# Second block's output product, residual, last norm, transposes and router: from one pass over both tiles to one pass per tile

## The chip, the cores and the metric

The kernel runs on one core of one Trainium2 chip. The metric is the device time of one execution in microseconds (us); a run counts with its median over several executions. TensorE (PE), VectorE (DVE), ScalarE (ACT), GpSimd (POOL) and SyncE (SP) each work through an instruction list of their own in order and meet through semaphores. Most of the work hands tiles between them.

## The reference, cut to what matters

Two model blocks follow one another on 512 tokens of width 1024. The second block, from its merged mixer output on, is what the change touches:

```
# second_block, one layer; x is [1, 512, 1024] float32
merged = sigmoid(gate_conv) * conv_o + sigmoid(gate_attn) * attn_o
h = h + merged @ w_out                        # output product and residual
xt = rms_norm_2(h, g_ffn)                     # the last norm ahead of the experts
g_logits = xt @ w_group + b_group             # router: 4 group columns
e_logits = xt @ w_expert + b_expert           # and 32 expert columns
...                                           # top 2 of 32 experts, each 1024 -> 512 -> 1024
```

`w_out` is [1024, 1024]; the router has 36 columns in all.

## The kernel before, in words

**Tiles and halves.** The 512 tokens are four tiles of 128. Two tiles make a half (`hf` 0 and 1), and every stage of the blocks is run by half. `H(t)` is the residual of tile `t` (128 tokens by 1024), `GC(k)` holds the merged mixer output transposed (128 channels by the 256 tokens of a half, k = 0..7), `r0` holds normed rows, and `GA(k)` the transposed normed rows that the router reads. `bank(b)` is one of eight PSUM banks of 512 columns.

**Interleaving.** `second_pe`, `second_act` and `second_dve` are generators, one for each engine. Half 0 of the second block runs beside the last pair of tiles of the first block's expert layer: `rows_pe` and its fellows walk through 64 steps, and `segs_at` says at which step each generator moves on to its next `yield`. On PE each of these steps (in the part at issue) is a sum of gathered rows (`sum_pe`, line 562, 16 or so matmuls), and POOL gathers 128 rows of `peer_v` by an indirect DMA for each (line 457), four to a step, into a ring of slots that the sums free. Half 1 of the second block runs alone after it (`for _ in second_pe(pe, 1): pass`), and after that come the routing (from line 2217) and the experts (from line 2335), which run in phases: no engine enters a phase before all have left the last.

**Order by name.** Each engine's steps have names in hand-written lists: `C_PE`, `C_ACT` and `C_DVE`. A step's place in its list is the value that its engine's semaphore has when it is done; `on_pe("o3")` waits for that value.

**The part at issue**, before: PE makes four output products `o0`..`o3` of 128x512 (8 matmuls each) in the order (columns 0 to 511, tile 0), (the same columns, tile 1), (columns 512 to 1023, tile 0), (these, tile 1). DVE adds each to `H` (line 1983). When a tile's second product is added (`h0`, `h1`), ACT squares and sums the row and takes the root (`rms`, lines 1777 and 1779); DVE takes the reciprocal (line 1884) and writes the normed row to `r0` (line 1991, `xn0`, `xn1`). PE waits for `xn1` and transposes both tiles together: 16 transposes of 128x128 into four banks (`turned_both`, line 1627). ACT copies them out in eight copies of 256 columns (line 1872, `x7_0`..`x7_7`). PE waits for the last copy and makes both tiles' router products (`lg0`, `lg1`), and DVE adds the bias (line 1996).

**Weights.** Weights are streamed by SP in the order of the list `stream`, 2 MB pieces for the most part, alternately into the two slots `w0` and `w1` (`wslot(i)`). SP issues piece i when piece i-2 has been used for the last time: `C_LAST_USE` names the PE step for each piece of a half. `w_out` is two pieces, columns 0 to 511 (called A below) and 512 to 1023 (B). A is issued when the last product of `w_attn_out` is done (`ma3`), B when the last one of `w_conv_out` is (`mc3`). The next half's first two pieces (of `w_in`) follow A and B. In half 1 one expert's down weights are put ahead of B in the same queue (`EXPERT_AT`, `expert_weights_sp`), and more expert weights stand behind it:

```
EXPERT_AT = {marks["attn_out1"]: 0, marks["out21"]: 1, marks["out21"] + 1: 2}
...
                if i in EXPERT_AT:
                    expert_weights_sp(sp, [EXPERT_AT[i]])
...
                sp.dma_start(dst, src).then_inc(sem(f"w_ready{i % 2}"), 16)
```

Matrix products go through the helper `matmuls`, whose line 196 is what the profile shows for them. One float32 matmul of the kernel gives two records there, one transpose gives one.

Of the kernel before, what the change touches and what calls it, by code (L numbers as in the profile page):

```python
# [7 lines left out]
ALU = mybir.AluOpType  # L8
ACT = mybir.ActivationFunctionType
AXIS_X = mybir.AxisListType.X  # L10

P = 128
D = 1024
# [15 lines left out]
def build_program(nc, A, out):  # L29
    ctx = ExitStack()  # L30
    with ctx:
# [49 lines left out]
        def wslot(i):  # L81
            return W[i % 2]
# [1497 lines left out]
        def by_head2(order):  # L1580
# [10 lines left out]
        C_PE = [(four("turn") + ["g0", "g1", "a0", "a1", "q0", "q1", "kk", "vv"] + heads  # L1591
                 + four("ma") + ["ln1", "ln2"] + four("mc") + four("o") + four("turn7_") + ["lg0", "lg1"])
                for heads in (apart(PE_HEADS), beside(PE_HEADS, 1))]
        C_ACT = [(["sq5_0", "rms5_0", "sq5_1", "rms5_1", "sq6_0", "rms6_0", "sq6_1", "rms6_1"] + [f"x6_{k}" for k in range(KD)]
                  + ["g0", "g1", "q0", "q1", "kk", "vv"] + heads + four("ysq") + ["lnrms", "silu"]
                  + ["sq7_0", "rms7_0", "sq7_1", "rms7_1"] + [f"x7_{k}" for k in range(KD)])
                 for heads in (apart(ACT_HEADS), [n for n in beside(ACT_HEADS, 3) if n[:2] != "ga"]
                               + four("ga") + four("sc"))]
        C_DVE = (["h5_0", "h5_1", "raw0", "raw1", "cv0", "cv1"]
                 + by_head2(((1, "sec"), (0, "fs"), (0, "fm"))) + four("ma") + ["cen", "nrm"] + four("mc")  # L1600
                 + ["h0", "h1", "xn0", "xn1", "lg0", "lg1"])
        c_pe, c_act, c_dve = by_half(C_PE), by_half(C_ACT), numbered(C_DVE)
        C_LAST_USE = ["g1", "a1", "q1", "vv", "gc1", "gc3", "ga1", "ga3", "ma3", "mc3", "o1", "o3"]

# [13 lines left out]
        def second_pe(pe, hf):  # L1618
# [135 lines left out]
            for g in range(4):  # L1754
                i = first + 10 + g // 2
                if g % 2 == 0:
                    w_arrived(pe, i)
                did(matmuls(pe, bank(g), lambda k: GC(k, (g % 2) * P, P), lambda k: wslot(i)[:, k, :], KD))
                yield
            yield  # L1760
            on_dve("xn1")
            turned_both(lambda t, k: mem("r0", t * D + k * P, P))
            yield
            on_act("x7_7")
            for i in range(2):
                did(matmuls(pe, bank(i, 0, NL), lambda k: GA(k, i * P, P), ROUTER, KD))
            yield

        def second_act(act, hf):
# [95 lines left out]
            for i in range(2):  # L1865
                on_dve(f"h{i}")
                rms(i, "7_", "r0")
            yield
            for k in range(KD):
                if k % 2 == 0:  # L1870
                    on_pe(f"turn7_{k // 2}")
                did(act.activation(GA(k), bank(k // 2, (k % 2) * 256, 256), ACT.Copy))
            yield
            yield
# [4 lines left out]
        def second_dve(dve, hf, link):  # L1879
# [93 lines left out]
            for b in range(4):  # L1973
# [5 lines left out]
                yield  # L1979
            for g in range(4):  # L1980
                t = 2 * hf + g % 2
                on_pe(f"o{g}")
                add = dve.tensor_tensor(H(t, 512 * (g // 2), 512), H(t, 512 * (g // 2), 512), bank(g), ALU.add)
                if g >= 2:
                    did(add)
                yield
            for i in range(2):
                t = 2 * hf + i
                on_act(f"rms7_{i}")
                rstd(t)  # L1990
                did(dve.scalar_tensor_tensor(mem("r0", t * D, D), H(t), mem("cols", COL_RSTD + t, 1), FFN_ROW, ALU.mult, ALU.mult))
            yield
            yield
            for i in range(2):
                on_pe(f"lg{i}")
                did(dve.tensor_tensor(LOGITS(2 * hf + i), bank(i, 0, NL), RB, ALU.add))
            yield
# [321 lines left out]
        def expert_weights_sp(sp, qs):  # L2319
            for q in qs:  # L2320
# [7 lines left out]
                if q == 5:  # L2328
                    sp.wait_ge(sem("c_dve"), c_dve(1, "lg1"))
                    sp.wait_ge(sem("c_act"), c_act(1, "x7_7"))  # L2330
                if q >= len(EREGS):
# [228 lines left out]
```

## Time and profile before

| what | value |
|---|---|
| median of 3 runs | 3019.09 us (3007.09 to 3020.22) |
| profiled execution, its own time | 3044.59 us |
| its span | 3042.9 us |
| PE busy in the span | 2276.7 us (75%) |
| DVE, ACT, POOL busy | 1551.5, 473.8, 1098.1 us |
| mean granted TensorE clock | 0.848 of full speed |

The profile is one execution under the hardware profiler, whose span runs from the first to the last record. Times in the rows count from the span's start. A number in square brackets behind a timeline row is how long the engine sat idle before it, and what ended that.

### The profile page before, as it was taken

What the parts mean: (1) busy time and instruction counts of PE and PEld (TensorE: products, weight loads), DVE (VectorE), ACT (ScalarE), POOL (GpSimd) and SP (SyncE); (2) the same over time, 40 slices, a digit from 0 to 9 for tenths busy, and PEclk for the clock granted to TensorE, in tenths of its full rate; (3) what the DMA queues carried; (4) which work ended last, traced back from release to release, by engine and by line L of the source; (5) the groups of instructions that cost most, each with busy time, mean ns of one, the idle gap of its engine ahead of it and who ended that gap; (6) DMA issues with size and microseconds to landing.
All of it is one profiled execution on the core that took longest, in us unless ns stands there. A gap on an engine that the chain in (4) does not pass through costs nothing.

```text
span 3042.9 us, 29697 instructions
## 1 busy us (share of the span) xinstructions
PE 2276.7 (75%) x11113; PEld 1284.6 (42%) x11113; DVE 1551.5 (51%) x3350; ACT 473.8 (16%) x786; POOL 1098.1 (36%) x1229
## 2 busy tenths in 40 slices
PE   6999485595557596457887267667798789999995
PEld 4676354342325342325643145333376533333331
DVE  3867698625854424953433875572135232333333
ACT  1212111110102410102510101110212111111111
POOL 1111355665642655642555653555400000000001
PEclk8999797897658797658888677778899889999997
DMA  8995699999996999996899989979754358989995
GB/s 320 345 338 194 218 393 373 351 379 372 352 356 254 361 370 369 343 353 246 311 363 348 370 334 356 333 277 365 291 215 140 137 220 327 412 336 405 412 415 194
DMA packets 266572, 977.45 MB, mean 321 GB/s; under 512 B 26173, under 2 KB 32421, under 8 KB 254151
## 3 DMA queue, kind: packets, MB, share of 16 engines
q0 software_dynamic: 169664, 615.13, 53.6%
q1 hardware_dynamic: 90480, 353.93, 30.2%
q10 hardware_dynamic: 6296, 6.57, 0.6%
q8 instruction: 89, 1.46, 0.2%
q14 instruction: 43, 0.35, 0.0%
HBM read 951.92 MB, written 23.63 MB: 321 GB/s over the span
## 4 chain that ended last, share of the span: by engine, by line
PE 56%; issue 13%; DVE 10%; DMA 9%; POOL 4%; another core or an unknown queue 4%; ACT 3%; SPq 1%; POOLq 0%; DVEq 0%; ACTq 0%
PE psum L196 27%; PE psum L2364 8%; PE psum L2346 4%; PE psum L562 4%; DMA arena<-in_peer_v_dram,arena 4%; PE psum L2383 4%; POOL arena L457 4%; DMA arena<-in_hgrn_w_in_dram 2%; DVE arena L469 2%; DMA arena<-in_ada_w_dram 2%; PE psum L1675 1%; PE psum L2340 1%; DVE arena L663 1%; PE psum L1451 1%
## 5 line engine op out<-in xcount | busy, mean ns | idle before, releaser
L196 PE MATMUL psum<-arena 128*128 128x256 f32 (+3 forms) x3784 | 1023.4, 427 | 169.9 <-issue 118.6
L196 PEld LDWEIGHTS psum<-arena 128*128 128x128 f32 x3784 | 721.1, 201 | 489.6 <-issue 365.5
L457 POOL DMA_INDIRECT arena<-in_peer_u_dram,arena x512 | 490.4, 958 | 460.7 <-DVE arena L469 217.7
L457 POOL DMA_INDIRECT arena<-in_peer_v_dram,arena x512 | 498.7, 974 | 394.8 <-PE psum L562 147.6
L469 DVE CUSTOM_DVE_ANT_0 arena<-arena,psum 128x1024 f32<-128x1024 f32 x512 | 592.6, 1216 | 74.5 <-DMA arena<-in_peer_u_dram,arena 58.3
L562 PE MATMUL psum<-arena 128*32 128x512 f32 x2048 | 319.4, 752 | 188.2 <-DMA arena<-in_peer_v_dram,arena 166.3
L2364 PE MATMUL psum<-arena 128*64 128x512 f32 x1088 | 240.8, 595 | 0.0
L562 PEld LDWEIGHTS psum<-arena 128*32 128x32 f32 x2048 | 68.1, 126 | 374.5 <-issue 367.7
L2458 POOL DMA_DIRECT2D y_slots<-arena x68 | 36.4, 535 | 517.8 <-DVE arena L2444 515.8
L2346 PE MATMUL psum<-arena 128*64 128x512 f32 x576 | 140.4, 610 | 6.6 <-DVE arena L2406 6.6
L2430 DVE TENSOR_TENSOR arena<-arena,psum 64x512 f32<-64x512 f32 x34 | 23.5, 691 | 236.8 <-ACT arena L2397 236.8
L2364 PEld LDWEIGHTS psum<-arena 128*64 128x64 f32 x1088 | 75.4, 137 | 138.7 <-issue 137.6
L2383 PE MATMUL psum<-arena 128*64 128x512 f32 x544 | 122.5, 592 | 0.0
L1895 DVE SCALAR_TENSOR_TENSOR arena<-arena 128x256 f32<-128x256 f32 x240 | 97.3, 478 | 0.0
L2397 ACT ACTIVATE arena<-psum 64x512 f32<-64x512 f32 x34 | 20.0, 589 | 482.0 <-PE psum L2364 482.0
L1451 PE MATMUL psum<-arena 128*128 128x256 f32 (+1 forms) x208 | 56.2, 440 | 49.0 <-DVE arena L1542 47.1
L663 DVE SCALAR_TENSOR_TENSOR arena<-arena 128x512 f32<-128x512 f32 x119 | 89.5, 752 | 4.2
L2450 POOL DMA_DIRECT2D arena<-in_g_final_dram x2 | 1.0, 512 | 249.8 <-issue 248.3
L611 POOL DMA_DIRECT2D arena<-in_ada_w_dram x20 | 18.6, 932 | 162.6 <-DVE arena L663 114.7
L777 PE MATMUL psum<-arena 128*128 128x128 f32 x112 | 23.0, 390 | 65.7 <-issue 46.4
L2383 PEld LDWEIGHTS psum<-arena 128*64 128x64 f32 x544 | 39.1, 137 | 77.6 <-issue 77.6
L1451 PEld LDWEIGHTS psum<-arena 128*128 128x128 f32 x208 | 45.9, 258 | 59.1 <-DVE arena L1542 50.1
(371 smaller groups left out, 2114.5 us busy)
## 6 DMA issues: line engine op xcount, KB each, us to landing
arena<-in_w_gate_dram SPq DMA_DIRECT2D x32, 2048.0 KB, 19.2
arena<-in_w_up_dram SPq DMA_DIRECT2D x32, 2048.0 KB, 10.3
arena<-in_w_down_dram SPq DMA_DIRECT2D x32, 2048.0 KB, 14.9
arena<-in_ada_w_dram POOLq DMA_DIRECT2D x20, 2048.0 KB, 11.0
arena<-in_hgrn_w_in_dram SPq DMA_DIRECT2D x16, 2048.0 KB
arena<-in_w_in_dram SPq DMA_DIRECT2D x14, 2048.0 KB
arena<-in_peer_w_q_dram SPq DMA_DIRECT2D x8, 2048.0 KB, 7.7
arena<-in_kv_w_dram SPq DMA_DIRECT2D x8, 2048.0 KB
```

The source lines that it names most:

```text
L196: last = pe.matmul(o, lhsT=lhs(k), rhs=rhs(k), start=start and k == 0, stop=stop and k == n - 1)
L457: pool.indirect_dma_start(RING(n, k), None, (U_TAB, V_TAB)[v], bass.IndirectOffsetOnAxis(ap=at, axis=0))\
L469: last = dve.tensor_tensor_reduce(out=row, in0=row, in1=bank(XB0, 0, D), scale=1.0, scalar=0.0, op0=ALU.mult, op1=ALU.add, accum_out=par_s ...
L562: last = pe.matmul(bank(ACC + half, 0, 512, parts=(32 * g, 32)), lhsT=mem("t", D + (s // 4 % 2) * 512 + (g * GR + s % 4) * 32, 32), rhs=RI ...
L663: ins = dve.scalar_tensor_tensor(MOD_ACC(j), MOD_W(j)[:, k, :], C_COL(k), MOD_ACC(j), ALU.mult, ALU.add)
L1451: last = pe.matmul(bank(ZB(h), o + w - min(w, wm), min(w, wm)), lhsT=mem("negtri" if m == n else "negones", 0, P), rhs=AW(hf, h, om, wm), ...
L1675: last = pe.matmul(bank(b, p * 256, 256, parts=(64 * a, 64)), lhsT=wslot(i)[:, k, a * 256 + (2 * b + p) * 64:a * 256 + (2 * b + p) * 64 + 64],
L1895: ins = dve.scalar_tensor_tensor(Y2(hf, c), CV(c, 256 * hf + i, 256), CCOL(c, i), Y2(hf, c), ALU.mult, ALU.add)
L2346: last = pe.matmul(bank(1, 0, 512, parts=half(n)), lhsT=PLACED(t), rhs=mem("r0", t * D + n * 512, 512), start=t == 0, stop=t == TT - 1, sk ...
L2364: last = pe.matmul(bank(2, 0, FF, parts=half(m)), lhsT=XBT[:, k, :], rhs=EW(e, m)[:, k, :], start=k == 0, stop=k == KD - 1, skip_group_che ...
L2383: last = pe.matmul(bank(4, 0, 512, parts=half(n)), lhsT=HT[:, k, :], rhs=EW(e, 2)[:, k, n * 512:(n + 1) * 512], start=k == 0, stop=k == NF ...
L2458: pool.dma_start(y_slots[bass.ds(g * SLOTS, SLOTS), m * 512:(m + 1) * 512], mem("w0", 1536, D // 2, parts=half(m)))\
```

## The change

PE makes the output products tile by tile: (tile 0, columns 0 to 511), (tile 0, 512 to 1023), (tile 1, 0 to 511), (tile 1, 512 to 1023). DVE adds tile 0's two products, norms tile 0, then adds and norms tile 1. PE still makes all four products first; then, for each tile: 8 transposes into two banks, two copies of 512 columns by ACT in place of eight of 256 for both tiles, and the router product of this tile. The step lists, the release of `w_in`'s first piece (`o2` in place of `o1`) and the wait of SP ahead of expert weights 5 (`x7_3`, still the last copy) follow suit. The number of `yield`s stays the same.

```diff
-                 + four("ma") + ["ln1", "ln2"] + four("mc") + four("o") + four("turn7_") + ["lg0", "lg1"])
+                 + four("ma") + ["ln1", "ln2"] + four("mc") + four("o") + ["turn7_0", "turn7_1", "lg0", "turn7_2", "turn7_3", "lg1"])
...
-                  + ["sq7_0", "rms7_0", "sq7_1", "rms7_1"] + [f"x7_{k}" for k in range(KD)])
+                  + [n for i in range(2) for n in (f"sq7_{i}", f"rms7_{i}", f"x7_{2 * i}", f"x7_{2 * i + 1}")])
...
-                 + ["h0", "h1", "xn0", "xn1", "lg0", "lg1"])
+                 + ["h0", "xn0", "h1", "xn1", "lg0", "lg1"])
...
-        C_LAST_USE = ["g1", "a1", "q1", "vv", "gc1", "gc3", "ga1", "ga3", "ma3", "mc3", "o1", "o3"]
+        C_LAST_USE = ["g1", "a1", "q1", "vv", "gc1", "gc3", "ga1", "ga3", "ma3", "mc3", "o2", "o3"]
...
             for g in range(4):
-                i = first + 10 + g // 2
-                if g % 2 == 0:
+                i = first + 10 + g % 2
+                if g < 2:
                     w_arrived(pe, i)
-                did(matmuls(pe, bank(g), lambda k: GC(k, (g % 2) * P, P), lambda k: wslot(i)[:, k, :], KD))
-                yield
-            yield
-            on_dve("xn1")
-            turned_both(lambda t, k: mem("r0", t * D + k * P, P))
-            yield
-            on_act("x7_7")
+                did(matmuls(pe, bank(g), lambda k: GC(k, (g // 2) * P, P), lambda k: wslot(i)[:, k, :], KD))
+                yield
             for i in range(2):
-                did(matmuls(pe, bank(i, 0, NL), lambda k: GA(k, i * P, P), ROUTER, KD))
+                on_dve(f"xn{i}")
+                for b in range(2):
+                    for j in range(4):
+                        last = pe.transpose(bank(2 * i + b, j * P, P), mem("r0", (2 * hf + i) * D + (4 * b + j) * P, P), ident)
+                    did(last)
+                yield
+                on_act(f"x7_{2 * i + 1}")
+                did(matmuls(pe, bank(2 * i, 0, NL), lambda k: GA(k, i * P, P), ROUTER, KD))
             yield
...
             for i in range(2):
                 on_dve(f"h{i}")
                 rms(i, "7_", "r0")
-            yield
-            for k in range(KD):
-                if k % 2 == 0:
-                    on_pe(f"turn7_{k // 2}")
-                did(act.activation(GA(k), bank(k // 2, (k % 2) * 256, 256), ACT.Copy))
-            yield
+                for b in range(2):
+                    on_pe(f"turn7_{2 * i + b}")
+                    did(act.activation(mem("r5", 2 * D + b * D + i * P, (256, 4), P), bank(2 * i + b, 0, 4, P), ACT.Copy))
+                yield
             yield
...
-            for g in range(4):
-                t = 2 * hf + g % 2
-                on_pe(f"o{g}")
-                add = dve.tensor_tensor(H(t, 512 * (g // 2), 512), H(t, 512 * (g // 2), 512), bank(g), ALU.add)
-                if g >= 2:
-                    did(add)
-                yield
             for i in range(2):
                 t = 2 * hf + i
+                for c in range(2):
+                    on_pe(f"o{2 * i + c}")
+                    add = dve.tensor_tensor(H(t, 512 * c, 512), H(t, 512 * c, 512), bank(2 * i + c), ALU.add)
+                    if c:
+                        did(add)
+                    yield
                 on_act(f"rms7_{i}")
                 rstd(t)
                 did(dve.scalar_tensor_tensor(mem("r0", t * D, D), H(t), mem("cols", COL_RSTD + t, 1), FFN_ROW, ALU.mult, ALU.mult))
...
-                did(dve.tensor_tensor(LOGITS(2 * hf + i), bank(i, 0, NL), RB, ALU.add))
+                did(dve.tensor_tensor(LOGITS(2 * hf + i), bank(2 * i, 0, NL), RB, ALU.add))
...
                 if q == 5:
                     sp.wait_ge(sem("c_dve"), c_dve(1, "lg1"))
-                    sp.wait_ge(sem("c_act"), c_act(1, "x7_7"))
+                    sp.wait_ge(sem("c_act"), c_act(1, "x7_3"))
```

## Rows read from the trace of the kernel before

**Rows 1.** The page: the chain that ended last, and a PE group of the expert phase.
```profile
PE 56%; issue 13%; DVE 10%; DMA 9%; POOL 4%; another core or an unknown queue 4%; ACT 3%; SPq 1%; POOLq 0%; DVEq 0%; ACTq 0%
...
L2364 PE MATMUL psum<-arena 128*64 128x512 f32 x1088 | 240.8, 595 | 0.0
```

**Rows 2.** Timeline of the part at issue in half 1 (start us, us, engine line).
```profile
2392.70 27.73 PE L196 MATMUL psum<-arena 128*128 128x512 f32 x64 [1.50 <-DVE arena L1978]
...
2415.49 1.28 ACT L1779 ACT_TABLE_LOAD   x1
...
2420.47 0.69 DVE L1983 TENSOR_TENSOR arena<-arena,psum 128x512 f32<-128x512 f32 x1 [6.18 <-PE psum L196]
...
2421.19 1.06 ACT L1777 ACTIVATE arena<-arena 128x1024 f32<-128x1024 f32 x1 [4.11 <-DVE arena L1983]
...
2424.24 3.62 PE L1627 MATMUL psum<-arena 128*128 128x128 f32 x16 [3.81 <-DVE arena L1991]
...
2428.60 4.81 PE L196 MATMUL psum<-arena 128*128 128x36 f32 x32 [0.75 <-ACT arena L1872]
...
2433.45 0.20 DVE L1996 TENSOR_TENSOR arena<-psum,arena 128x36 f32<-128x36 f32 x1 [2.64 <-PE psum L196]
```

**Rows 3.** The costliest ACT groups by shape: a copy of 512 columns out of PSUM.
```profile
L1802 ACT ACTIVATE arena<-psum 128x512 f32<-128x512 f32 x4 | 2.4, 597 | 41.9 <-remote 25.4 <-PE psum L196 16.4
```

**Rows 4.** Windows in half 1: busy time of PE, PEld, DVE, ACT, POOL, then PEclk, DMA share, GB/s.
```profile
2392.00:2396.00 4.00, 3.30 (x8) 1.63 (x9) 0.65 (x1) 0.00 (x0) 0.00 (x0) 1.00 0.99 332
...
2424.00:2428.00 4.00, 3.62 (x16) 3.27 (x16) 0.18 (x1) 2.08 (x7) 0.00 (x0) 0.57 0.00 0
```

**Rows 5.** SP's queue in half 1: when each transfer was issued.
```profile
2391.23 0.34 SPq L2333 DMA_DIRECT2D arena<-in_w_down_dram  x1
2391.61 0.44 SPq L148 DMA_DIRECT2D arena<-in_w_out_dram  x1
2392.14 3.16 SPq L2333 DMA_DIRECT2D arena<-in_w_gate_dram  x1
```

**Rows 6.** DMA issues of the same moments: KB each, us from issue to landing.
```profile
arena<-in_w_down_dram SPq DMA_DIRECT2D x1, 2048.0 KB, 7.7
...
arena<-in_w_gate_dram SPq DMA_DIRECT2D x1, 2048.0 KB, 17.0
```

**Rows 7.** Timeline of the part at issue in half 0, beside the gathered sums.
```profile
2121.09 0.37 SPq L148 DMA_DIRECT2D arena<-in_w_out_dram  x1
...
2122.57 9.46 PE L196 MATMUL psum<-arena 128*128 128x512 f32 x16 [6.60 <-DVE arena L1978]
...
2133.82 7.13 PE L196 MATMUL psum<-arena 128*128 128x512 f32 x16
...
2140.98 0.37 SPq L148 DMA_DIRECT2D arena<-in_w_in_dram  x1
...
2164.00 1.97 PE L1627 MATMUL psum<-arena 128*128 128x128 f32 x16
...
2174.93 3.64 PE L562 MATMUL psum<-arena 128*32 128x512 f32 x16 [8.96 <-DMA arena<-in_peer_v_dram,arena]
...
2178.50 3.97 PE L196 MATMUL psum<-arena 128*128 128x36 f32 x32
...
2182.40 3.35 PE L562 MATMUL psum<-arena 128*32 128x512 f32 x16
```

**Rows 8.** SP's DMA queue at 2135.0 to 2135.5, 2135.5 to 2136.0, 2162 to 2164 (packets, MB, share).
```profile
q1 hardware_dynamic: 10, 0.02, 9.6%
...
q1 hardware_dynamic: 1, 0.00, 0.1%
...
q1 hardware_dynamic: 359, 0.74, 99.7%
```

**Rows 9.** POOL's timeline in half 0: first and last of the 8 last gathers.
```profile
2160.94 0.94 POOL L457 DMA_INDIRECT arena<-in_peer_v_dram,arena  x1 [4.24 <-PE psum L562]
...
2169.88 0.94 POOL L457 DMA_INDIRECT arena<-in_peer_v_dram,arena  x1 [0.30 <-issue]
```

## The prediction, made before the kernel ran

> **What bounds the kernel now.** I read the page first. The chain that ended last is PE's for 56% of the span, and the experts' largest PE group shows no idle time before it at all, so what the experts wait for is only their start: time saved or lost ahead of them moves the end one for one [rows 1]. Then I read the timeline of the part at issue twice, because it runs in two surroundings. In half 1 it stands alone on the path. Four output products take 27.73 us without a gap. Then PE waits 3.81 us for the last add, the square, the root and the norm of tile 1, transposes both tiles in 3.62 us, waits 0.75 us for the last copy and makes both router products in 4.81 us; the last bias add starts at 2433.45 and ends at 2433.65 [rows 2]. From the end of the products (2392.70 + 27.73 = 2420.43) that is a tail of 13.2 us. Nothing of tile 0 is in it but its half of the transposes, copies and router. In half 0 the same steps lie between sums of gathered rows, and there the gathers set the pace: the sum at 2174.93 was released by a gather's DMA [rows 7]. I then read SP's queue, because the new order asks for `w_out`'s piece B one product earlier.
>
> **The change in half 1: the tail.** Let P be the end of the four products. Tile 1's chain up to its square is as before: add, h1 at P + 0.73. But ACT now has tile 0's two copies ahead of tile 1's square. PE makes tile 0's 8 transposes at P. At full clock one takes 1.97 / 16 = 0.123 us (half 0 [rows 7]), so four are done at P + 0.49 and eight at P + 0.98. A copy of 512 columns takes 0.597 us [rows 3], so the copies run from P + 0.55 to P + 1.15 and on to P + 1.75; the square starts there and not at P + 0.76 (2421.19 [rows 2]): the change itself makes it 1.0 us late. From square to transposes it was 2424.24 - 2421.19 = 3.05 us [rows 2], and nothing in that stretch changes, so tile 1's transposes start at P + 4.80. Tile 0's router product lies in the wait ahead of them: 3.97 / 2 = 1.99 us [rows 7], from P + 1.8 to P + 3.8. Then four transposes (0.49), the wait for the semaphore (0.06), two copies (1.2, the second limited by the first) bring P + 6.6, the router 1.99 and the bias add 0.06 + 0.2: P + 8.9. The tail shrinks from 13.2 to 8.9 us, a gain of 4.3. At half clock (a transpose 3.62 / 16 = 0.226; a tile's router product 2.8, what is left of 4.81 behind one of 1.99 [rows 2]) the same sum gives P + 11.2, a gain of 2.0. I take 4.3: PE's gaps are 1.0 us and less there, and the gap of 1.50 us ahead of the products left the clock at 1.00 [rows 2, 4].
>
> **The change in half 1: piece B.** Before, B was used from the third product on, at 2392.70 + 2 x 6.93 = 2406.6. Now the second product needs it, at 2399.6. B was issued at 2391.61, behind an expert's down weights (2391.23) and ahead of its gate weights (2392.14) [rows 5]. All are 2 MB. The down weights landed 7.7 us after issue, at 2398.9, the gate weights 17.0 us after issue, at 2409.1 [rows 6]; B has no landing of its own in the rows, but as the middle one of three equal pieces it landed about halfway, at 2404.0. That was 2.6 us of slack, and is now a stall of 4.4 us. Bounds: not before the down weights (stall 0), not after the gate weights (stall 9.5). What is queued behind the stall on PE is everything: three products, tile 0's norm, the tail. And the stall has a second price. After PE sat idle for 3.81 us the clock fell from full speed (2.4 GHz) to the lower level (1.2 GHz): 0.57 in the window of the transposes [rows 4]. After 6.60 us of idling a product of 16 records took 9.46 us where a product at full clock takes 7.13 [rows 7]: 2.3 us more. A stall of 4.4 lies between these two idle times; I take 2.3, bounds 0 and 2.3.
>
> The Trainium skill ("TensorE: Matmul & The Clock Gate", part 1) says that the clock is gated down after an idle stretch and comes back after sustained work, and its table for kernel authors warns against idle gaps of PE between bursts. The trace agrees, with 0.57 behind the gap of 3.81 us; without that rule's cost the sum below would be 2.3 us lower.
>
> Sum for half 1: +4.4 +2.3 -4.3 = +2.4 us. Bounds: -4.3 (B in time) and 9.5 + 2.3 - 2.0 = +9.8.
>
> **The change in half 0.** B was issued at 2121.09 and shares the engines with gathers; the last but one of SP's packets of B moved before 2135.5 and a single one after it [rows 8], so it landed at about 2135.8. The third product started at 2142.7, now the second one needs it at 2133.82 [rows 7]: 2.0 us of stall. The sums after it, and with them the last gathers that their slots release, slide by as much: eight gathers issued from 2160.94 to 2169.88, one every 1.24 us [rows 9]. Further, the release of `w_in`'s first piece moves from `o1` (2140.98 [rows 7]) to `o2`, about 2149.8 + 2.0; its own use is far off (half 1), but it now runs against gathers. What such a piece does is seen when the second one was issued at `o3`: for two microseconds SP's queue had 99.7% of the engines and the gathers nothing [rows 8]. Before, the first piece did this while few gathers were waiting. A piece of 2 MB holds the engines 5.1 us (half the distance from 2398.9 to 2409.1). I charge 1 us, for the gathers that it meets belong to a sum three steps later, and keep 0 and 5.1 as bounds. Against that, half of the router, 3.97 / 2 = 2.0 us, leaves the gap between the last two sums (2174.93 to 2182.40 [rows 7]), since tile 0's router now comes a step earlier, where PE waits 9 us for a gather anyway. The transposes of tile 0 take 1.0 us one sum earlier, before that same wait, and cost nothing; without that wait they would cost it. Sum: +2.0 +1.0 -2.0 = +1.0. Bounds: -2.0 (the stall is absorbed in the wait for gathers, w_in costs nothing) and 2.0 + 5.1 - 0 = +7.1.
>
> **What costs nothing.** `yield`s are as many as before, so no other stage is moved. DVE's norm of tile 0 now stands ahead of the adds of tile 1; the same chain took 3.81 us for tile 1, and for tile 0 there is a table load of 1.28 us ahead of the root [rows 2]: 5.1 us after `o1`, while the third product takes 6.9 and covers it. Expert weights 5 wait for the same last step and come earlier or later with it.
>
> **Sum.** +2.4 +1.0 = +3.4 us against the profiled execution's own 3044.59 us (span 3042.9), that is +0.11%, and the same on the median, 3019.1 + 3.4 = 3022. I take 0.5% (15 us) as what a measurement of this kernel can tell from no change; its three runs span 13 us.
>
> **Rivals.**
> (a) B arrives in time, or its wait costs nothing: the change is what it looks like, a shorter tail. -4.3 in half 1, up to -2.0 in half 0: 3019.1 - 6.3 = 3013. For it: I have no landing row for B. Against it: three equal pieces in one queue, and B the second. That is not 0.5% either; even a tail of nothing would give only 13.2 us. The Trainium skill ("DMA: Bandwidth & Descriptors", section on queues, rings and completion order) says that each engine consumes a queue's descriptors in ring order; by that B can't pass the down weights. The landings at 7.7 and 17.0 us fit it, and the sum doesn't rest on it.
> (b) Slower: the last gathers of half 0. Both pieces of `w_in` are now issued at `o2` and `o3`, next to the last twelve gathers. If each holds them up in full, that is 2 x 5.1 = 10.2 us, and PE, idle longer than before, restarts at half clock, 2.3 more: 12.5 us beyond my forecast, 3035. For it: 99.7% of the engines for SP's queue [rows 8]. Against it: the second piece did so before already and is in the 9 us wait of today. It decides (over 15 us in all) only when the gathers come over 11.6 us later than in my sum.
> (c) No change in the place of the work: PE's stall takes back exactly the tail, and half 0 hides everything; 3019. It can't be told from the forecast by the time, only by the rows.
>
> **Chances.** The forecast 0.67 (its own range 3010 to 3032, half of the runs' spread either way and the bounds of the stall), (a) 0.15, (b) 0.08, (c) 0.10. The range for 8 in 10: from (a) with the runs' spread of some 6 us below, 3007, to just short of (b), 3033. Faster by over 0.5%: only by luck of (a), 0.03. Slower by over 0.5%: most of (b), 0.06. Within 0.5%: 0.91.
>
> **What the profile after will show.** In half 1: one product of about 6.9 us, an idle time of PE of 4.4 us released by `w_out`'s DMA, the next products first at half clock, then DVE's last add 1 us ahead of ACT's square; tile 1's transposes x8 4.8 us after the products' end; the last bias add 8.9 us after it, not 13.2. ACT's copies as 128x512, x8 in all in place of x16. In half 0: about 2 us idle after the first product, and only x16 router records between the last two sums. It would be wrong if PE does not wait for `w_out` in half 1 (then (a)), if the gap costs no clock, or if the last sum of the first block moves by over 5 us (then (b)).

## The result: 0.5 to 0.7% slower

| | median | lowest to highest | runs |
|---|---|---|---|
| before | 3019.09 us | 3007.09 to 3032.12 | 5 |
| changed | 3036.90 us | 3027.39 to 3042.13 | 5 |

The ratio is 1.0068, with a 95% interval of 1.0043 to 1.0092: 17.8 us slower, where 3022 us and no measurable change were forecast. Two later measurements of the same changed kernel, each against the kernel before in the same job, gave 1.0047 (1.0032 to 1.0061) and 1.0057 (1.0039 to 1.0075). The profiled execution of the changed kernel took 3038.59 us (span 3036.9), close to its median. That of before, on which the prediction rests, took 3044.59 us, 25 us over its median, so the two profiles can't be compared by their ends: by these the changed kernel would be 6 us faster. They can be compared by stretches.

The timeline of the changed kernel in half 1, PE, ACT, DVE and SP's queue (start us, us, engine line), to be held against [rows 2, 5]:

```profile
2377.99 0.34 SPq L2332 DMA_DIRECT2D arena<-in_w_down_dram  x1
2378.37 0.44 SPq L148 DMA_DIRECT2D arena<-in_w_out_dram  x1
...
2379.46 7.13 PE L196 MATMUL psum<-arena 128*128 128x512 f32 x16 [1.50 <-DVE arena L1978]
...
2391.25 23.91 PE L196 MATMUL psum<-arena 128*128 128x512 f32 x48 [4.65 <-DMA arena<-in_w_out_dram]
...
2415.00 1.04 PE L1764 MATMUL psum<-arena 128*128 128x128 f32 x8
...
2415.64 1.08 ACT L1872 ACTIVATE arena<-psum 128x512 f32<-128x512 f32 x2 [10.69 <-PE psum L1764]
2416.61 1.06 ACT L1779 ACTIVATE arena<-arena 128x1024 f32<-128x1024 f32 x1
2416.77 1.98 PE L196 MATMUL psum<-arena 128*128 128x36 f32 x16 [0.74 <-ACT arena L1872]
...
2419.65 1.09 PE L1764 MATMUL psum<-arena 128*128 128x128 f32 x8 [0.90 <-DVE arena L1990]
...
2421.48 3.63 PE L196 MATMUL psum<-arena 128*128 128x36 f32 x16 [0.74 <-ACT arena L1872]
2425.15 0.20 DVE L1995 TENSOR_TENSOR arena<-psum,arena 128x36 f32<-128x36 f32 x1 [5.44 <-PE psum L196]
2425.37 0.33 SPq L2332 DMA_DIRECT2D arena<-in_w_down_dram  x1
```

The reader sees the stall (4.65 us, released by `w_out`'s DMA), three products that take 23.91 us where three at full clock take 20.8, the copies of 512 ahead of the square, and tile 1's router product at 3.63 us although tile 0's took 1.98. The windows over the tail say why: the granted clock falls in it.

```profile
2416.00:2420.00 4.00, 2.36 (x20) 2.21 (x20) 1.55 (x3) 2.05 (x5) 0.00 (x0) 1.00 0.00 0
2420.00:2424.00 4.00, 3.26 (x19) 3.02 (x18) 0.00 (x0) 1.08 (x2) 0.00 (x0) 0.66 0.00 0
2424.00:2428.00 4.00, 1.11 (x6) 0.97 (x5) 2.24 (x20) 1.50 (x2) 0.00 (x0) 0.50 0.46 111
```

In half 0 the stall is larger than in half 1. The timeline of PE and SP in the changed kernel, against [rows 7]:

```profile
2103.89 7.13 PE L196 MATMUL psum<-arena 128*128 128x512 f32 x16
...
2121.09 8.74 PE L196 MATMUL psum<-arena 128*128 128x512 f32 x16 [8.21 <-DMA arena<-in_w_out_dram]
...
2131.61 7.13 PE L196 MATMUL psum<-arena 128*128 128x512 f32 x16
...
2138.77 9.29 SPq L148 DMA_DIRECT2D arena<-in_w_in_dram  x2
...
2140.52 7.13 PE L196 MATMUL psum<-arena 128*128 128x512 f32 x16
```

PE stands still for 8.21 us for piece B, which was issued at 2102.14, when the last product of `w_conv_out` (`mc3`) was done, and landed 18.9 us later. 2.0 us of stall were forecast. Behind the stall the product takes 8.74 us and not 7.13.

### The profile page after: what moved, and what is told of

Same layout as the page of the kernel before. It is cut to its first block, busy times and chain, and to the rows that moved or that the text cites. A ratio compares the mean times of both kernels' runs of the same rounds, so it can differ in the third digit from the quotient of the medians.

```text
span 3036.9 us, 29689 instructions
## 1 busy us (share of the span) xinstructions
PE 2270.9 (75%) x11113; PEld 1276.4 (42%) x11113; DVE 1551.9 (51%) x3350; ACT 472.6 (16%) x778; POOL 1093.9 (36%) x1229
## 4 chain that ended last, share of the span: by engine, by line
PE 54%; issue 13%; DVE 12%; DMA 10%; another core or an unknown queue 3%; ACT 3%; POOL 3%; SPq 1%; POOLq 0%; DVEq 0%; ACTq 0%
PE psum L196 26%; PE psum L2363 8%; PE psum L2345 5%; PE psum L2382 4%; DMA arena<-in_peer_v_dram,arena 4%; PE psum L562 3%; POOL arena L457 3%; DVE arena L469 3%; DMA arena<-in_hgrn_w_in_dram 3%; DMA arena<-in_ada_w_dram 2%; PE psum L1675 1%; DVE arena L1895 1%; PE psum L2339 1%; PE psum L1451 1%
```

## Measures used below

Most kernels' executions within one job spread by 15 to 38 us in group I of the table and by 6 to 17 us in group II; the two groups of jobs differ by 160 us in the stages ahead of the part at issue (piece A of half 0 is issued at 2058.13 us in one profile of before and at 1898.37 in another). So ratios are within one job, and traces are compared by three stretches between SP's issues, worked out from each profile's timeline:

- *half 0*: from the issue of piece A in half 0 to that of piece A in half 1;
- *half 1*: from the issue of piece B to the next issue behind the last bias add (expert weights 5);
- *start*: from there to the issue of expert weights 7, which waits for the first expert.

From that last point to the end all kernels take 563.2 to 564.0 us, but for the two with half of piece B (see below). In c1, d3 and f4 piece B is issued some 0.4 us earlier than in the others against the work around it, so half 1 comes out 0.4 us too long there. *Wait for B there* is PE's idle time ahead of the first product that needs piece B in half 0.

| profile | group | half 0 | wait for B there | half 1 | start |
|---|---|---|---|---|---|
| before | I | 290.1 | 0 | 42.06 | 45.65 |
| a1_before_again | I | 286.8 | 0 | 42.08 | 45.63 |
| a3_before_look | I | 276.5 | 0 | 42.07 | 45.65 |
| a4_before_look | II | 281.3 | 0 | 44.36 | 48.98 |
| changed | I | 286.6 | 8.2 | 47.00 | 48.05 |
| a2_after_again | II | 287.6 | 8.4 | 46.38 | 46.29 |
| a5_after_third | II | 290.7 | 8.1 | 47.41 | 46.57 |
| b1_new_half0 | I | 290.5 | 2.1 | 42.08 | 45.63 |
| b2_new_half1 | I | 288.5 | 0 | 46.24 | 46.30 |
| c1_half1_b_first | I | 287.1 | 0 | 40.24 | 48.26 |
| d1_order_only | II | 292.6 | 8.1 | 52.17 | 45.67 |
| d2_tail_only | II | 277.3 | 0.6 | 39.86 | 48.25 |
| d3_change_b_first | II | 286.8 | 8.1 | 40.24 | 48.51 |
| e1_order_half0 | I | 288.6 | 1.9 | 44.35 | 48.97 |
| f1_before_busy_route | I | 275.3 | 0 | 41.92 | 45.11 |
| f2_tail_busy | I | 280.0 | 0 | 37.39 | 43.33 |
| f3_tail_busy_again | II | 277.2 | 0.7 | 37.39 | 43.34 |
| f4_change_b_first_busy | II | 289.2 | 8.5 | 37.77 | 43.32 |
| h1_change_half_b | II | 284.4 | 5.8 | 46.88 | 48.04 |
| h2_before_half_b | II | 278.1 | 0 | 42.06 | 45.63 |

Half 0 has two courses in these profiles, and they begin ahead of its first output product, which the change doesn't touch. In six of them (before, a1, b1, b2, c1, e1, all of group I) PE stands idle for 4.8 to 6.7 us there, B is issued 57 to 60 us after A, and the first product takes 8.9 to 9.9 us. In the fourteen others there is no such idle time, B is issued 50 to 55 us after A, and the product takes 7.13 us. I call the first the *late* course. What brings it about is not shown. The prediction rests on a profile of the late course. With the old order, half 0 takes 286.8 to 290.1 us in the late course and 275.3 to 281.3 in the other; with the new one, 288.6 and 290.5 against 286.6 to 292.6 (all of piece B loaded). So by these profiles the new order costs 1 to 2 us in the late course and some 11 in the other.

## The experiments

### The kernel before against itself

No edit. 

> The kernel before, unchanged, timed against itself. The profiled execution of before took 3044.59 us, 25 us over its median of 3019.09, so it may not be the usual execution. Theory of a real loss: ratio 1.000 with an interval of at most 0.3% to either side, and a profile near 3019 us whose last stretches of half 0 (from w_out's piece A to the last sum) differ from the first profile. Rival, the +17.8 us are spread between executions: the ratio here is itself off 1 by 0.4% or more.

Measured: 0.9988 (0.9965 to 1.0011), 12 runs against 35. So the comparison itself is good to about a quarter of a per cent there, and a median of five executions can be off by several us. The profile's half 0 was 3.3 us shorter than in the first profile, half 1 the same to 0.02 us.

### Each half alone

The edit makes every changed place depend on the half:

```diff
+        ORDER_2, TAIL = (True, False), (True, False)      # half 1 alone: (False, True) twice
...
-                i = first + 10 + g // 2
+                c, t = (g % 2, g // 2) if ORDER_2[hf] else (g // 2, g % 2)
+                i = first + 10 + c
```

> Both parts of the change (order of the products, tail by tile) in half 0 alone, half 1 as before. Theory H0 (the loss sits in half 0, where PE waited 8.2 us for w_out's piece B): +10 to +15 us, 0.3 to 0.5%. Theory H1 (it sits in half 1 and the experts' start): within 3 us of before.

> Both parts in half 1 alone, half 0 as before. From the two profiles, half 1 from w_out's second piece's issue to SP's next issue took 47.38 us after and 42.44 us before (+4.9), and the first steps of the experts +2.4 at half clock. Theory H1: +7 us or more (0.25%). Theory H0: +5 to +7 us, the smaller part.

Measured: 1.0018 (1.0001 to 1.0035) for half 0, 1.0021 (1.0003 to 1.0040) for half 1. Both intervals only just exclude no change; by the medians each half has its share, and the sum is 0.39%, or 12 us. Neither theory that puts the loss in one half stands. Half 0's share is smaller than expected, and its profile is of the late course, with a wait for B of 2.1 us. Half 1's +4.2 us in its stretch and +0.65 in the start agree with its ratio.

### Piece B ahead of the expert's weights, half 1 alone

```diff
-                if i in EXPERT_AT:
+                if i in EXPERT_AT and i != marks["out21"] + 1:
                     expert_weights_sp(sp, [EXPERT_AT[i]])
...
                 sp.dma_start(dst, src).then_inc(sem(f"w_ready{i % 2}"), 16)
+                if i == marks["out21"] + 1:
+                    expert_weights_sp(sp, [EXPERT_AT[i]])
```

> As the run before (change in half 1 alone), but SP issues w_out's piece B ahead of the expert's down weights. If the queue position makes the stall, B lands about 7.8 us after issue, at the end of the first product: PE's wait falls from 4.65 us to under 1 us, the second product has no half clock, and the kernel is 6 to 7 us faster than with the change in half 1 as it is, so about 4 us faster than before (-0.13%). If the transfer alone is too slow for one product, the wait stays at 2 us or more.

Measured: 0.9997 (0.9976 to 1.0018), and 1.0021 in the same job without the edit. PE's four products run without a gap, as the timeline of this kernel shows:

```profile
2385.89 0.37 SPq L148 DMA_DIRECT2D arena<-in_w_out_dram  x1
...
2387.36 27.73 PE L198 MATMUL psum<-arena 128*128 128x512 f32 x64 [1.51 <-DVE arena L2008]
...
2414.93 1.04 PE L1773 MATMUL psum<-arena 128*128 128x128 f32 x8
...
2419.59 1.97 PE L1773 MATMUL psum<-arena 128*128 128x128 f32 x8 [0.91 <-DVE arena L2014]
...
2422.24 3.63 PE L198 MATMUL psum<-arena 128*128 128x36 f32 x16 [0.69 <-ACT arena L1891]
2425.91 0.20 DVE L2032 TENSOR_TENSOR arena<-psum,arena 128x36 f32<-128x36 f32 x1 [6.27 <-PE psum L198]
```

The queue's order makes the stall in half 1. But the kernel isn't the hoped 4 us faster than before: half 1 is 1.8 us shorter by the table and 2.2 from the same point, since tile 1's transposes (1.97) and router product (3.63) run at the lower clock, and the start is 2.6 us longer.

### Order and tail taken apart

`order_only` keeps `turned_both`, the eight copies and the common router; `tail_only` keeps the old order of the products:

```diff
+        ORDER_2, TAIL = (True, True), (False, False)      # order_only; tail_only: the reverse
```

> The changed kernel, timed again. The parts alone gave +0.18% (half 0) and +0.21% (half 1); their sum is 0.39%, or +12 us. Theory of two stalls that add: 1.002 to 1.006. Rival, the first measurement's 1.0068 holds and the parts strengthen each other: 1.006 or more. In the profile: PE waits for w_out's piece B in both halves, about 4.5 us in half 1 and 2 to 8 us in half 0.

> The new order of the products (with DVE's norm of tile 0 ahead of tile 1's adds), but transposes, copies and router as before, for both tiles together. Theory: the order carries all of the loss. Half 1: a stall of 4.5 us, some 2 us of half clock behind it, and the tail of 13.2 us from the last product to the last bias add as before: 48.5 to 49 us from SP's issue of B to its next issue, against 42.1 before; the first expert steps as before (45.6 us from that issue to the next one). Ratio 1.003 to 1.006. Rival: the per-tile tail is what costs, and this is within 0.1% of before.

> The old order of the products, with norm, 8 transposes, two copies of 512 and router product tile by tile in both halves. No wait for piece B in either half. Half 1: the tail is 11.2 us and not 13.2 (its last router product runs at half clock, as in the changed kernel), so 40.0 us from B's issue to the next; the first expert steps 0.7 to 2.6 us longer at half clock, as in the three profiles with this tail. Ratio 0.998 to 1.001. If the tail itself carried the loss: 1.003 or more.

> The whole change, with w_out's piece B issued ahead of the expert's down weights in half 1. Half 1 alone this way was 0.9997. Theory: what is left is half 0's part, 1.001 to 1.003, about 6 us faster than the changed kernel of the same job. Rival, the stall in half 1 is not what costs: as slow as the changed kernel.

Measured in one job: changed 1.0047 (1.0032 to 1.0061); order alone 1.0066 (1.0054 to 1.0079); tail alone 0.9992 (0.9981 to 1.0003); the whole change with B first 1.0026 (1.0016 to 1.0035). The order carries the whole loss and more; the tail gives a part back, 6.7 us between the medians of order alone and changed, though the interval of the tail alone reaches no change. With B first the kernel is 5.1 us faster than changed, where 6 were expected. The last two kernels differ in half 0's order alone but for B's place in half 1, which then costs nothing there (39.86 and 40.24 us): their medians are 9.1 us apart, their half 0 9.5 us. The order alone cost half 1 more than expected, 52.17 us against 48.5 to 49: its 32 router records took 7.04 us, at the lower clock throughout, and not 4.81. The stall isn't shown to be the reason: a4_before_look and e1_order_half0, with half 1 as before and no stall in it, have the same 7.04.

```profile
2239.39 23.92 PE L196 MATMUL psum<-arena 128*128 128x512 f32 x48 [4.49 <-DMA arena<-in_w_out_dram]
...
2271.54 7.04 PE L196 MATMUL psum<-arena 128*128 128x36 f32 x32 [0.75 <-ACT arena L1900]
```

The same router products in e1_order_half0:

```profile
2414.26 7.04 PE L196 MATMUL psum<-arena 128*128 128x36 f32 x32 [0.75 <-ACT arena L1900]
```

### The order in half 0 alone

```diff
+        ORDER_2, TAIL = (True, False), (False, False)
```

> The kernel before, one look, so that there is a trace of it from the same chip as the runs beside it. From SP's issue of w_out's piece A in half 0 to its issue of piece A's successor B in half 1 the parts run so far took 326.3 us with the change and 317.3 us with the tail alone, on one chip. If the order alone makes that difference, before is at 317 to 319 us there.

> The new order of the products in half 0 alone, everything else as before. Theory: in half 0 piece B takes 15 to 19 us from issue while gathers share the engines, is wanted 8.8 us after its issue, and PE waits for it for up to 8.4 us; the sums and the gathers behind it slide. Ratio 1.002 to 1.004 (half 0's share), and a wait of PE for w_out of 2 to 8.4 us in the trace. Rival: the gathers hide it, within 0.05% of before.

Measured: 1.0023 (0.9999 to 1.0047), as expected in size, but the interval reaches no change. The wait for B was 1.9 us, in a profile of the late course. From piece A in half 0 to piece B in half 1 the profile of before took 316.5 us, but in group I, while the two stretches that it was to be held against (326.3 with the change, 317.3 with the tail alone) were of group II. The profile of before in group II (a4_before_look) settles it: 318.9 us, so the order makes most of that difference. One finding stands against a theory that I had formed: here half 1 is exactly as before, and yet it took 44.35 us and the start 48.97. So a start at the lower clock needs no new tail; it comes and goes between executions of one and the same code (a4_before_look: 44.36 and 48.98; the five other profiles with all of half 1 and the routing as before: 42.06 to 42.08 and 45.63 to 45.65). The new tail without a stall ahead of it had the long start in three profiles of three (48.25 to 48.51), so that it has a part in it isn't ruled out.

### Matmuls into the idle times

`busy` issues matmuls whose result nobody reads: 6 ahead of the counting products, 5 behind them, 2 ahead of the first expert; for `tail_busy` also four of 256 columns in half 1's tail.

```diff
+        def busy(pe, n, cols=512):
+            for _ in range(n):
+                pe.matmul(bank(7, 0, cols), lhsT=ident, rhs=H(0, 0, cols), start=True, stop=True)
...
+            busy(pe, 6)
             pe.wait_ge(sem("chosen"), 1)
...
+                    if hf and i:
+                        busy(pe, 2, 256)
                     on_dve(f"xn{i}")
...
+                    if hf:
+                        busy(pe, 1, 256)
                     on_act(f"x7_{2 * i + 1}")
```

> The kernel before, with 13 more matmuls of 512 columns (their results unused, in a PSUM bank that nothing reads) put into PE's idle times in the routing and ahead of the first expert. If the lower clock after idling is what makes these steps long, the counting products take 2.3 + 1.0 us and not 4.45 + 1.9, and the first placing products 3.65 us and not 5.0: 4 to 5 us faster, 0.9985. If the added matmuls only delay: slower by up to 3 us.

> The old order of the products with the tail tile by tile in both halves, and added matmuls whose results are unused: the 13 of the run before, and in half 1's tail four of 256 columns in PE's waits. If the clock falls because PE does too little there: tile 1's router product takes 2.0 us and not 3.63, no half clock in the first expert steps, and the sum is 8 to 10 us faster than before, 0.997. If the clock falls anyway: as the tail alone, 0.999.

Measured: routing alone 0.9989 (0.9970 to 1.0008), unclear, with 0.5 us less in the start and not 4 to 5; with the tail 0.9976 (0.9956 to 0.9997). With routing alone the counting and first placing products were as short as hoped (2.31 and 3.65 us), but the six added matmuls ahead of them cost time themselves. They began at the lower clock (0.50 from 2420 to 2424) and outlasted the wait that they were to fill: the counting products began 7.6 us after the bias add and not 5.8. With the tail filled too, the clock was at 1.00 when they began, and they fitted (5.7 us). These are the six matmuls (L1625 is `busy`), with routing alone and with the tail:

```profile
2421.79 7.49 PE L1625 MATMUL psum<-arena 128*128 128x512 f32 x12 [0.53 <-POOLq L182]
...
2396.74 5.39 PE L1625 MATMUL psum<-arena 128*128 128x512 f32 x12 [0.53 <-POOLq L182]
```

PE's timeline of `tail_busy` behind the products:

```profile
2387.75 1.04 PE L1777 MATMUL psum<-arena 128*128 128x128 f32 x8
...
2389.52 1.98 PE L196 MATMUL psum<-arena 128*128 128x36 f32 x16 [0.30 <-ACT arena L1897]
2391.33 1.11 PE L1625 MATMUL psum<-arena 128*128 128x256 f32 x4
2392.40 1.09 PE L1777 MATMUL psum<-arena 128*128 128x128 f32 x8
...
2394.23 1.97 PE L196 MATMUL psum<-arena 128*128 128x36 f32 x16 [0.30 <-ACT arena L1897]
...
2402.18 2.42 PE L2260 MATMUL psum<-arena 128*128 128x32 f32 x20
...
2414.04 3.65 PE L2390 MATMUL psum<-arena 128*64 128x512 f32 x16 [0.18 <-DVE arena L2451]
```

Tile 1's router product takes 1.97 us and not 3.63, the counting products 2.42 and not 4.45, the first placing products 3.65 and not 4.99 to 6.63. Half 1 is 4.7 us shorter than before, the start 2.3: 7.0 us, against a median that is 8.7 lower.

### Half of piece B

In half 0 only columns 0 to 255 of piece B are loaded; the products read the other 256 as the slot has them, so half 0's tokens get other values there.

```diff
+                if i == marks["out20"] + 1:
+                    dst, src = dst[:, :, 0:256], src[:, :, 0:256]
```

> The kernel before, one look, for a trace from the same chip: 315 to 330 us from SP's issue of w_out's piece A in half 0 to its issue of piece B in half 1, no wait of PE for w_out.

> The changed kernel once more, beside the two runs after it: 1.004 to 1.006 of before; waits of PE for piece B in both halves.

> The changed kernel, but in half 0 only columns 0 to 255 of w_out's piece B are loaded (1 MB instead of 2; the products still read all 512 columns of the slot, so tokens of half 0 get other values in 256 columns). If the wait for B is half 0's cost: B lands 8 to 10 us after issue, the wait in half 0 falls below 2 us, and the kernel takes 0.2 to 0.3% less than the changed one, 1.002 to 1.003 of before. If the order costs half 0 in another way (w_in's later release, the norm between the adds): within 0.1% of the changed kernel.

> The kernel before, with the same 1 MB less in half 0 (the same 256 columns are not loaded). It never waits for B, so what it gains is what the smaller transfer gives by leaving the engines to the gathers: 0 to 2.6 us (1 MB at 400 GB/s), 0.9992 to 1.000.

Measured: changed 1.0057, the changed kernel with half of B 0.9989 (0.9976 to 1.0002), before with half of B 0.9932 (0.9908 to 0.9956). Read as they are, these would say that 1 MB less gives 16 us even where nobody waits for it. They can't be read so: the other values send the tokens to other experts. The expert phase from weights 7 on took 547.84 and 548.18 us and not 563.4, and its groups hold 1056 records (this kernel's own row) where [rows 1] has 1088, one block of slots fewer:

```profile
L2400 PE MATMUL psum<-arena 128*64 128x512 f32 x1056 | 233.8, 595 | 0.0
```

With 15.6 us added to each, before with half of B is level with before (2867.9 us against 2868.2) and the changed kernel with half of B is 3.9 us faster than the changed one (2881.6 against 2885.5). The wait in half 0 fell from 8.1 to 5.8 us, not below 2: half the bytes in as many, half as long, pieces landed only a little sooner (16.5 us after issue, where the whole took 18.9), and not 8 to 10 us after it, as expected. This agrees with a cost of the wait, but it is a small lever.

### Half 0's order by itself

```diff
+        ORDER_2, TAIL = (True, True), (True, True)        # with B first and busy; beside tail_busy
```

> The old order, the tail tile by tile, and the added matmuls, timed again: 0.9976 before, so 0.996 to 0.999. If the first result was luck: 0.999 to 1.001.

> The whole change with the new order in both halves, piece B ahead of the expert's down weights in half 1, and the same added matmuls. Half 1 then costs nothing for the order, so the distance to the run beside it is half 0's order alone: 5 to 10 us by theory (the wait for piece B), 0.2 to 0.35%. If half 0's wait is covered by the gathers: within 0.1% of the run beside it.

Measured in one job: `tail_busy` 0.9964 (0.9950 to 0.9978), the other 1.0008 (0.9998 to 1.0019), 11.7 us apart by their medians. Their half 1 and start are the same to 0.4 us, their half 0 differs by 12.0 us (277.2 and 289.2). Here are the two PE timelines over `o0` and the product behind it, first with the new order, then with the old one:

```profile
1947.70 7.13 PE L198 MATMUL psum<-arena 128*128 128x512 f32 x16
1954.77 1.92 PE L564 MATMUL psum<-arena 128*32 128x512 f32 x16
1965.20 9.41 PE L198 MATMUL psum<-arena 128*128 128x512 f32 x16 [8.51 <-DMA arena<-in_w_out_dram]
1974.54 1.92 PE L564 MATMUL psum<-arena 128*32 128x512 f32 x16
```

```profile
1946.58 7.13 PE L196 MATMUL psum<-arena 128*128 128x512 f32 x16
1953.64 1.92 PE L562 MATMUL psum<-arena 128*32 128x512 f32 x16
1955.49 7.13 PE L196 MATMUL psum<-arena 128*128 128x512 f32 x16
1962.56 1.92 PE L562 MATMUL psum<-arena 128*32 128x512 f32 x16
1965.20 7.13 PE L196 MATMUL psum<-arena 128*128 128x512 f32 x16 [0.72 <-DMA arena<-in_w_out_dram]
```

Piece B lands at the same point of both traces, but with the old order a whole product and a sum lie ahead of its first use, and PE waits 0.72 us and not 8.51. From B's issue to `o3` the new order takes 10.1 us more: 7.8 of wait and 2.3 of half clock behind it. So most of half 0's 12.0 us are there; 0.3 lie ahead of B's issue and 1.7 between `o3` and the last sum. By 9.5 and 12.0 us in the profiles, and 9.1 and 11.7 by the medians, the order costs half 0 some 9 to 12 us in group II.

## Why the prediction was wrong

**What bounds the kernel** held: the experts' phase takes the same in all kernels, and what is lost ahead of it is lost at the end.

**Half 1, the stall** (forecast 4.4 us): 4.65, 4.68 and 5.13 us in the three profiles of the changed kernel, 4.5 in three others, at the place and by the DMA named. The landing taken from equal pieces was right to 1.0 us, and B first in the queue took the stall away.

**Half 1, the clock behind the stall** (forecast 2.3): 23.27 to 23.92 us for three products of 6.93, so 2.5 to 3.1.

**Half 1, the tail** (forecast from 13.2 to 8.9 us, gain 4.3): from the products' end (2391.25 + 23.91 = 2415.16) to the bias add's end (2425.35) it took 10.2, a gain of 3.0; without a stall ahead of it 11.0, a gain of 2.2. The order of the steps was as forecast: ACT's square 1 us late, transposes 4.5 us behind the products. I took the full clock because the gaps are 1.0 us and less. That reason failed: the clock fell all the same between 2420 and 2424, and tile 1's router product cost 3.63 us and not 1.99. The prediction's other sum, at half clock, gave 11.2. The stretch came out at +4.3 to +5.3 us against before's 42.07, not at +2.4; but before itself took 44.36 in one profile.

**The experts' start** was not in the sum. It was 0.6 to 2.4 us longer in the three profiles of the changed kernel. Since two profiles with half 1 as before have it at 48.97 and 48.98 us too, I can't charge it to the change; how often each state comes with each kernel stays open.

**Half 0** (forecast +1.0) is the step that failed: the term "2.0 us of stall", and with it the claim that the stretch is worth 1 us. It measured 8.1 to 8.4 us in the three profiles of the changed kernel and 8.1 to 8.5 in three others, and the half costs 9 to 12 us where it was isolated. I read both ends of the stall from the one profile of before: B landed 14.7 us after its issue, and the new order's second product could have begun 12.7 us after it. That profile is of the late course, and for that course 2.0 was right: the two profiles of the new order in it waited 1.9 and 2.1 us, as here in `new_half0`:

```profile
2115.24 9.17 PE L196 MATMUL psum<-arena 128*128 128x512 f32 x16 [6.26 <-DVE arena L2006]
...
2128.37 8.83 PE L196 MATMUL psum<-arena 128*128 128x512 f32 x16 [2.11 <-DMA arena<-in_w_out_dram]
```

In the other course both ends move. PE isn't late, so the second product could begin 10.7 us after B's issue, 2.0 earlier, and B lands 18.8 to 19.3 us after it, some 4 later: 8.2 in place of 2.0. While B was under way the gathers moved 5.2 MB in the changed kernel, 3.0 MB in before and 2.9 MB in `new_half0`. In the profile of before SP's queue had most of the engines from 2123 to 2125, soon after B's issue (q1 is SP's, q0 the gathers'; packets, MB, share):

```profile
q1 hardware_dynamic: 293, 0.60, 82.9%
q0 software_dynamic: 36, 0.09, 11.8%
```

As soon after the issue, at 2104 to 2106, SP's queue moved 0.09 MB in the changed kernel. Its DMA queues at 2108 to 2110 show what B meets when gathers are dense:

```profile
q0 software_dynamic: 146, 0.54, 65.5%
q1 hardware_dynamic: 148, 0.30, 38.8%
```

and those of `new_half0` at 2116 to 2118, where the wait was 2.1 us, the other case:

```profile
q1 hardware_dynamic: 348, 0.71, 98.6%
q0 software_dynamic: 5, 0.01, 1.1%
```

The Trainium skill ("DMA: Bandwidth & Descriptors", section on queues, rings and completion order) says that an engine goes round between the queues it has work for and drains a whole packet of one, some 9 to 17 descriptors, before it turns to the next. Whether its packets are the profile's isn't shown; that the two queues take turns, the trace bears out. The profile's packets come out in equal numbers, 146 and 148, while the gathers' are 3.7 KB long on average (0.54 MB in 146) and B's 2.0 KB (0.30 MB in 148), so B gets 0.30 of 0.84 MB, about a third. That is a price by packets. Half of B, in as many packets of 1 KB, pays the same one: at 1960 to 1962 of that profile the numbers are again equal, and it gets 0.17 of 0.80 MB.

```profile
q0 software_dynamic: 169, 0.63, 80.0%
q1 hardware_dynamic: 165, 0.17, 24.5%
```

**The rivals.** (a) did not happen. (b), slower by half 0, had the right half and sign but another mechanism: it put the cost on `w_in`'s later release, and this can hold only a part of the 1.7 us behind `o3`. The point from which it was to decide, gathers 11.6 us later than in my sum, was all but reached where piece B's wait was long (12.0 us against the 1.0 of the sum). (c) is out.

**The range** (3007 to 3033) treated half 0's stall as known to a few tenths, from a row of one execution, and had no bound for a B that lands later. In half 1 the gate weights' landing, 17.0 us after issue, was such a bound. In half 0 a B that takes 19 us would have added 6 us of stall and 2.3 of half clock: 3030, and the runs' spread on top. The measured 17.8 us lie within what the parts give outside the late course: 9 to 12 for half 0, 4.3 to 5.3 for half 1, 0.6 to 2.4 for the start. The chance of 0.06 for slower by over 0.5% was too low.

## What to carry to other kernels

When a new order of loops asks for a weight piece earlier, read when it lands in every place where the loop runs, and in more than one profile: a landing beside other traffic is a range, not a number, and so is the moment when the piece is needed. An order that uses one weight piece for all tiles before it touches the next gives the transfer time; a tail tile by tile can be had without giving that up (`tail_busy`, 0.9976 and 0.9964, is the fastest version here, ahead of both kernels). A short chain of small products on the path was cheaper with unread matmuls in its gaps, where these began at the full clock and didn't outlast the gap; where they began at the lower clock they took 7.49 us and not 5.39 and gave almost nothing.

## What the runs showed of the hardware

- Gaps of 0.3 us with filler between kept the granted clock (1.00 from 2388 to 2396 in `tail_busy`); with waits of 0.7 to 0.9 us between short products it fell (1.00 between 2416 and 2420, 0.66 between 2420 and 2424), though no gap was over 1 us. The Trainium skill ("TensorE: Matmul & The Clock Gate", part 1) tells of a kernel whose short idle times between groups of matmuls made the clock go back and forth. This trace agrees in that the clock fell behind such idle times, with 3.63 us for a product that takes 1.98 at the full clock.
- The same code in the tail of half 1 took 4.81 or 7.04 us for its router products, and at the start of the experts 45.65 or 48.97 us, with the first placing products at 5.0 or 6.62 us: two courses of the clock, in different executions.
- 2 MB in 2 KB packets took 18.8 to 20.3 us beside dense gathers, 14.6 to 15.1 in the late course, and an estimated 5.1 us with little beside it, from the landings in half 1 that the forecast's sum used. 1 MB in as many packets of 1 KB took 16.5 us beside dense gathers.
